# VectorE normalises the next pair of heads directly behind its maxima, in both attentions of a two-block network

## What is computed, cut to what matters

```python
# first block, attention "c": sliding window, one extra logit per head (sink)
logits = q k^T / 8 + band_bias            # masked outside the window
probs  = softmax([logits, sink])[..., :-1]
o      = probs v
# second block, attention "f": causal, biased by cumulated log forget gates
s = q k^T / 8 + cum[q] - cum[k]           # masked above the diagonal
o = softmax(s) v
```

## Time and profile before

| what | value |
|---|---|
| median of 3 runs | 3520.7 us (3520.23 to 3520.75) |
| the profiled execution | 3519.47 us |
| its span, first to last instruction | 3517.7 us |
| mean granted TensorE clock | 0.973 |
| TensorE busy | 3297.4 us (94%) |
| VectorE busy | 2092.7 us (59%) |
| ScalarE busy | 1515.8 us (43%) |

### The profile page before, as it was taken

The page is one execution under the profiler, slowest core; times in us unless marked ns, Lnnn a source line. Parts: engine busy times, 40 slices in busy tenths (PEclk is TensorE's granted clock), DMA queues, the critical chain, the costliest instruction groups (busy, mean ns, idle before and its releaser), DMA issues.

```text
span 3517.7 us, 54647 instructions
## 1 busy us (share of the span) xinstructions
PE 3297.4 (94%) x21910; PEld 3047.1 (87%) x21910; DVE 2092.7 (59%) x3174; ACT 1515.8 (43%) x2095; POOL 28.8 (1%) x44
## 2 busy tenths in 40 slices
PE   7888887899999997999887999999999999999998
PEld 7878777899999996989877988888888888888886
DVE  4445886755555546666335468967677566666665
ACT  4434333444444433444323454454444544444444
POOL 0000000000000000000000000000000000000000
PEclk9989999999999998999988999999999999999999
DMA  9323333454554452433213556666666866666653
GB/s 278 125 92 125 140 141 120 150 192 179 181 187 181 179 188 83 180 136 140 100 61 120 181 180 207 212 207 209 226 224 230 302 242 239 241 242 244 244 218 138
DMA packets 108254, 638.71 MB, mean 182 GB/s; under 512 B 11616, under 2 KB 28160, under 8 KB 38960
## 3 DMA queue, kind: packets, MB, share of 16 engines
q1 hardware_dynamic: 100368, 591.44, 47.1%
q0 software_dynamic: 7472, 44.57, 3.6%
q10 hardware_dynamic: 240, 0.25, 0.0%
HBM read 597.42 MB, written 38.80 MB: 181 GB/s over the span
## 4 chain that ended last, share of the span: by engine, by line
PE 85%; DVE 9%; ACT 2%; issue 2%; DMA 1%; DVEq 1%; ACTq 0%; SPq 0%
PE bank L375 14%; PE bank L358 13%; PE bank L360 13%; PE bank L359 13%; PE bank L376 7%; PE bank L996 7%; PE bank L995 7%; PE bank L994 7%; DVE dacc L1060 3%; DVE wlo L343 2%; PE bank L963 2%; PE bank L497 1%; ACT whi L337 1%; PE bank L494 1%; DMA raw<-stream 1%
## 5 line engine op out<-in xcount | busy, mean ns | idle before, releaser
L343 DVE TENSOR_TENSOR wlo<-raw,whi 128x1024 fp32r<-128x1024 f32 x1056 | 1286.8, 1225 | 1210.2 <-ACT whi L337 1199.5
L337 ACT CAST whi<-raw 128x1024 fp32r<-128x1024 f32 x1056 | 1104.2, 1048 | 1358.6 <-PE bank L360 833.0
L358 PE MATMUL bank<-xboth,whi 128*128 128x256 f32 x3312 | 953.0, 288 | 79.7 <-DVE wlo L343 55.5
L359 PE MATMUL bank<-xboth,whi 128*128 128x256 f32 x3312 | 943.2, 285 | 0.0
L360 PE MATMUL bank<-xboth,wlo 128*128 128x256 f32 x3312 | 942.8, 285 | 0.0
L375 PE MATMUL bank<-xboth,whi 128*128 128x512 f32 x2048 | 727.0, 399 | 0.0
L358 PEld LDWEIGHTS bank<-xboth,whi 128*128 128x128 f32 x3312 | 642.5, 194 | 88.4 <-DVE wlo L343 46.9
L359 PEld LDWEIGHTS bank<-xboth,whi 128*128 128x128 f32 x3312 | 642.3, 194 | 0.7
L360 PEld LDWEIGHTS bank<-xboth,wlo 128*128 128x128 f32 x3312 | 641.8, 194 | 0.0
L376 PE MATMUL bank<-xboth,wlo 128*128 128x256 f32 x2048 | 573.1, 280 | 0.0
L375 PEld LDWEIGHTS bank<-xboth,whi 128*128 128x128 f32 x2048 | 384.6, 188 | 89.7
(11 more groups left out here) (348 smaller groups left out, 3050.8 us busy)
## 6 DMA issues: line engine op xcount, KB each, us to landing
raw<-stream SPq DMA_DIRECT2D x528, 1024.0 KB, 4.8
up_activations<-ust SPq DMA_DIRECT2D x128, 128.0 KB, 5.1
gate_matrix<-gstage POOLq DMA_DIRECT2D x8, 2048.0 KB, 14.6
gslice<-gate_matrix POOLq DMA_DIRECT2D x8, 2048.0 KB, 10.7
uin<-up_activations SPq DMA_DIRECT2D x32, 512.0 KB, 5.6
relative_band<-cband POOLq DMA_DIRECT2D x1, 3072.0 KB, 37.3
xraw<-xt SPq DMA_DIRECT2D x1, 2048.0 KB, 7.7
cbias<-relative_band POOLq DMA_DIRECT2D x1, 2048.0 KB, 20.4
```

Of the source, the lines that this page charges most:

```text
L337: nc.scalar.copy(whi[b.half][:, k, :], raw[b.raw][:, k, :]).then_inc(hi_done, 1)
L343: nc.vector.tensor_tensor(wlo[b.half][:, k, :], raw[b.raw][:, k, :], whi[b.half][:, k, :].bitcast(f32), ALU.subtract).then_inc(lo_done, 1)
L358: nc.tensor.matmul(o, whi[b.half][:, k, :], rhi[:, r, :], start=i == 0, stop=False)
L359: nc.tensor.matmul(o, whi[b.half][:, k, :], rlo[:, r, :], start=False, stop=False)
```

## The change

The normalisation becomes a function, `scaled(c)`. It is called once for pair 0 behind `maxima(0)`, and then, in the turn of pair c, for pair c+1 behind `maxima(c + 1)`, ahead of `beside(c, 0)`. Before, it stood at the head of its own turn, behind everything of the turn before. Nothing changes on the other engines, and no instruction is added or taken out.

```diff
-            maxima(0)
-            for c in range(WC):
+            def scaled(c):
                 for par in range(2):
                     den = small[:, 8 * par + 4:8 * par + 6]
                     dve.wait_ge(sem("att_exp"), exps_before(name) + 4 * c + 2 * par + 2)
...
                     nc.vector.tensor_scalar(prob[par][:, 0, :], prob[par][:, 0, :], den[:, 0:1], None, ALU.mult)
                     nc.vector.tensor_scalar(prob[par][:, 1:3, :], prob[par][:, 1:3, :], den[:, 1:2], None,
                                             ALU.mult).then_inc(sem("att_prob"), 1)
+            maxima(0)
+            scaled(0)
+            for c in range(WC):
                 if c + 1 < WC:
                     maxima(c + 1)
+                    scaled(c + 1)
                 beside(c, 0)
                 for par in range(2):
                     p0, p1 = 64 * par, 64 * par + 64
```

## The result

Four runs of the changed kernel have a median of 3467.06 us (3466.13 to 3468.18), four of the kernel before 3520.47 us. The ratio is 0.9847, 95% interval 0.9835 to 0.9859: 53.4 us less. The forecast was 3465.5 us, with a range of 3456 to 3477. The profiled execution took 3467.08 us with a span of 3465.3 us, 52.4 us less than the span before.

What follows compares the result with a forecast made beforehand. TensorE was taken to bound the kernel, through its waits and slow clock. Gains of 39.9 us in c and 15.3 in f sum to 55.2, from 3519.47 to 3464.3; with 1.2 for the median, 3465.5 us, range 3456 to 3477.

Steps and rivals of the forecast that it cites:

- What bounds the kernel: TensorE, busy 94% of the span; a gain must come out of its waits or its slow clock.
- c: Attention c: transposes follow the block directly, no TensorE wait left, full clock, pairs of 16.45 us; 39.9 us gained.
- T: The start of a pair's transposes on TensorE.
- A: The start of the block that follows the next scores on TensorE.
- The cover in VectorE's queue: In c, the normalisation, 1.9 us in all, fits VectorE's 3.02 us idle time ahead of the split, 0.9 us to spare.
- The forecast's last part: Signs expected in the profile after, among them about 1.1 us idle ahead of VectorE's L343 instead of 3.02.
- f: Attention f: wait shrinks from 3.22 to 2.0 us, output copies late next; 8.5 us plus 6.8 of clock, 15.3 us.
- the number of falls: In f, half of the pairs were taken to lose clock after the 2.0 us wait, at 1.9 us a pair.
- The second rival: f's clock falls in every pair as now: gain 8.5 us, time 3472.3 us, chance 0.20.
- the third: A new wait in c from ScalarE crowded in the gate blocks: c keeps only 20 us, 3485 us, chance 0.08.
- the fourth: No effect: the convolution stage behind c and the blocks behind f take the gain back, 3520 us, chance 0.02.
- the fifth: Slower: VectorE, waiting for late exponentials, holds split, `x1` and output copies; 3530 us, chance 0.03.

Runs made afterwards that it cites:

- the kernel with five matmuls: The changed kernel plus 5 unused matmuls of 256 columns in TensorE's wait ahead of the transposes of pairs 1 to 7 in f: 3456.78 us.

## Why the prediction was right, step by step

**What bounds the kernel.** Right: the gain came from the waits of L508 for L551 and the falls behind them. How near the sum came is partly luck, as the terms show.

**c.** Forecast 39.9 us, measured 44.6 up to pair 7's products with v (301.11 to 256.51). The terms, by the windows:

| term | forecast | measured |
|---|---|---|
| pairs 1 to 6 | 34.8 | 133.45 - 96.73 = 36.7 |
| pair 0 | 3.4 | 22.51 - 17.77 = 4.7 |
| pair 7 | 1.7 | 8.13 - 6.40 = 1.7 |
| start of pair 0's transposes | 0 | 137.02 - 135.61 = 1.4 |

The mechanism is as written: T follows the block, and `att_o` is early. The way from T to A was 3.4 in the sum and is 3.09 (169.51 to 172.60), which makes 0.3 us in each of six pairs. One reading was off and changed nothing: `att_prob` is not there 13 us ahead of the new T, but 9.5 (160.03 to 169.51); the 13 were counted to the old T.

In pair 0 the way from A to the next T shrank by 3.4 us, from 16.44 to 13.04, as forecast. The other 1.3 us there and the 1.4 before it are chance: TensorE's instructions up to A are the same in both kernels, and the clock fell there twice before and once after. The traces of the other runs show how far it scatters. In all eleven the instructions up to there are the same, and pair 0's T lies anywhere from 134.76 to 137.64 us, the way from it to A takes 4.70 to 6.07. The changed kernel's second trace has pair 0 at 18.54 us instead of 17.77.

**The cover in VectorE's queue.** Right: 0.84 us to spare, forecast 0.9. The forecast's last part gave 1.1 for the same idle time.

**f.** Forecast 15.3 us, measured 11.6: pair 0 1.1 (16.76 to 15.62), pairs 1 to 6 10.6, pair 7 nothing (7.92 to 8.05, where 1.6 was forecast, since it fell too). The wait was to be 2.0 us and is 2.07; a pair without a fall was to be 14.9 us and is 14.96. The term that was mis-sized is the number of falls: half of them was taken, and six of seven came. The second rival (each pair falls, 8.5 us) priced the falls too high: it kept the 1.9 us a pair of the long waits, while behind 2.07 us a fall costs 16.61 - 14.96 = 1.65. With six falls at 1.65 the forecast's own sum, 22.1 at full clock, gives 12.2, near the 11.6 measured. So the forecast for f had too few falls, each at too high a price, and the two errors partly cancel. The forecast's own range for two to five falls was also wider than its terms give: at 1.94 us a fall they make 3462.6 to 3468.4, not 3461 to 3470.

The Trainium skill's rule on short idles (TensorE: Matmul & The Clock Gate, section "A second HAM failure mode: psum-queue depth-cycling": frequent short idles between groups of matmuls make the clock swing) was the better guide to the count at 2.07 us, where six of seven fell. The seven waits of 1.5 us in the kernel with five matmuls, without a fall, do not agree with it.

**Between and behind.** The forecast let every us of c and f reach the end. Of 56.2 us (44.6 + 11.6) 52.4 did. The two stretches that lost most, before, after, and the first of them once more in the changed kernel's second trace:

```profile
538.85:675.83 136.98, 110.19 (x827) 107.36 (x826) 90.84 (x101) 57.66 (x72) 2.90 (x4) 0.91 0.35 125
...
1847.38:3517.70 1670.32, 1634.50 (x8980) 1419.49 (x8978) 1072.43 (x1740) 767.08 (x1075) 12.50 (x18) 0.99 0.61 216
```
```profile
494.38:633.59 139.21, 112.38 (x828) 109.11 (x827) 91.12 (x102) 57.64 (x72) 3.28 (x4) 0.89 0.35 123
...
1793.95:3465.30 1671.35, 1635.52 (x8980) 1421.40 (x8978) 1072.62 (x1740) 766.73 (x1075) 12.47 (x18) 0.99 0.61 216
```
```profile
494.27:631.66 137.39, 110.57 (x827) 107.71 (x827) 91.04 (x102) 57.66 (x72) 3.70 (x4) 0.91 0.34 124
```

The norms behind the convolution took 2.2 us more and run at 0.89 instead of 0.91. The same kernel's second trace has only 0.4 us more and 0.91, with the same four waits of TensorE in all three (14.4, 7.3, 3.5 and 1.6 us), so most of this loss is not of the change's making. Over the eleven traces, none of which changes anything there, the stretch takes 136.6 to 140.1 us. All that follows f's last products with v lost 1.0, with the same one wait of 6.8 us at its start; the run with c alone changed, whose f is the old one, took 0.6 us more there too (1670.97). The errors, +4.7 in c, -3.7 in f and -3.8 around them, leave 2.8 us between the 55.2 of the sum and the span's 52.4. Of these, 2.7 in c and most of the 2.2 in the norms are scatter between traces. The median came out 1.6 us above the forecast, nearer than its terms did: that closeness is luck, the mechanism is not.

**The other rivals.** A crowded ScalarE (the third) did not show: two pairs with gate blocks, 217.87 to 250.11, take 16.12 us each, as the mean of the six does (96.73 / 6). A gain given back (the fourth) was wrong but for those 4 us. The slower case (the fifth) needed the exponentials 4 us later; the run with the normalisation behind `beside` shows the price of its mechanism, VectorE's copies held back by 1.3 us: f's gain was gone. Its 20 us for the clock behind a wait of 7 us are not shown, since no run has such a wait ahead of f's transposes.

## What to carry to other kernels

When a wait's releaser is moved forward, look for the second semaphore in the same place: here the bank's release, `att_o`, took over in f at 1.16 us less, and moving that as well was worth twice as much as moving the first (25.0 us against 12.5). Price a TensorE wait with what the clock does behind it: a third of c's gain was clock, and a fifth of f's. Work that others wait for goes ahead of work that is needed only two blocks later, and each attention has to be looked at for itself, since the same order is free in one and dear in the other.

## What the runs showed of the hardware that was not expected

The step from no fall to a fall is narrow in this loop: seven waits of 1.5 us brought none, seven of 2.07 us six. The same pairs fell, and pair 4 did not, when f alone was changed and in the changed kernel's second trace (98.02 us for pairs 1 to 6 in both, against 98.06). A stage that no edit touches can differ by 3 us from one trace to the next, so a term of that size is not to be read from two traces alone. And filling a wait with useless matmuls is a gain by itself: 364 of them made the kernel before faster by 22 us.
